# Gated linear attention layer: state products handed over two heads at a time, z units behind the last reads, weight parts in another order

## The reference, cut to what matters

```python
q, k, v, z, g_low = split(xn @ w_in)
log_a = log_sigmoid(g_low @ w_gate_up + b_gate) / 16
q_dec = q * dk ** -0.5 * exp(bcum); k_inv = k * exp(-bcum); k_dec = k * exp(b_last - bcum)
o_intra = tril(q_dec @ k_inv.T) @ v
def step(state, (qd, kd, vv, dec)):
    o = qd @ state
    state = state * dec[:, None] + kd.T @ vv
o = rms_norm(o_intra + o_inter, o_gain)
x = x + (o * silu(z)) @ w_out
```

## Time and profile before

| | us |
|---|---|
| median of 3 runs | 1286.72 |
| lowest, highest | 1285.8, 1289.21 |
| the profiled execution | 1288.8 |
| its span | 1287.1 |
| TensorE busy | 1108.6 (86%) |
| VectorE busy | 647.1 (50%) |
| ScalarE busy | 441.5 (34%) |
| granted clock of TensorE, mean | 0.961 |

### The profile page before, as it was taken

One profiled execution on the slowest core, in us unless ns is written; L12 is line 12 of the kernel. 1 busy time (PEld: TensorE's weight loads), 2 busy tenths in 40 slices (PEclk: granted clock), 3 DMA queues, 4 the chain that ended last, 5 costly groups with the idle time before them and its releaser, 6 DMA issues.

```text
span 1287.1 us, 19719 instructions
## 1 busy us (share of the span) xinstructions
PE 1108.6 (86%) x8083; PEld 817.1 (63%) x8083; DVE 647.1 (50%) x1279; ACT 441.5 (34%) x693; POOL 8.3 (1%) x36
## 2 busy tenths in 40 slices
PE   8999889897676758585858999999999989989998
PEld 8999767543131313130414789897779979868897
DVE  6886578420101111020203777767467966666685
ACT  5554334100000000000003556546356663255563
POOL 1000000000000000000000000000000000000000
PEclk9999999899898989898989999999999989899999
DMA  9576345999999999999998974354325530056600
GB/s 297 156 254 211 117 164 196 385 409 409 410 409 410 410 410 410 410 409 410 409 410 316 290 228 136 127 187 139 132 67 182 174 103 4 1 131 191 219 17 33
DMA packets 121045, 314.66 MB, mean 244 GB/s; under 512 B 17155, under 2 KB 19450, under 8 KB 120714
## 3 DMA queue, kind: packets, MB, share of 16 engines
q1 hardware_dynamic: 117904, 310.78, 65.9%
q0 software_dynamic: 352, 2.11, 0.4%
q10 hardware_dynamic: 2714, 0.71, 0.3%
HBM read 312.52 MB, written 1.06 MB: 244 GB/s over the span
## 4 chain that ended last, share of the span: by engine, by line
PE 59%; DMA 28%; DVE 7%; ACT 4%; issue 2%; SPq 1%; ACTq 0%; DVEq 0%
DMA ring<-in_w_up 18%; DMA ring<-in_w_down 10%; PE bank L2329 8%; PE bank L2322 7%; PE bank L2326 7%; PE bank L2308 6%; PE bank L2304 6%; PE bank L2311 6%; PE bank L2626 3%; PE bank L2649 2%; DVE w_l L1234 1%; PE bank L2237 1%; PE bank L2611 1%; PE bank L2732 1%; ACT w_h L694 1%
## 5 line engine op out<-in xcount | busy, mean ns | idle before, releaser
L1234 DVE TENSOR_TENSOR w_l<-ring,w_h 128x1024 fp32r<-128x1024 f32 x204 | 246.4, 1221 | 83.7 <-ACT w_h L694 82.3
L694 ACT ACTIVATE w_h<-ring 128x1024 fp32r<-128x1024 f32 x204 | 213.7, 1057 | 168.6 <-PE bank L2311 85.1
L2626 PE MATMUL bank<-ring,cm 128*32 128x512 f32 x880 | 135.4, 745 | 102.7 <-DMA ring<-in_w_gate 61.3
L2626 PEld LDWEIGHTS bank<-ring,cm 128*32 128x32 f32 x880 | 27.8, 120 | 208.6 <-DMA ring<-in_w_up 78.9
L2322 PE MATMUL bank<-w_h,hnT_h 128*128 128x512 f32 x480 | 135.1, 403 | 6.9 <-ACT hnT_h L789 2.7
L2329 PE MATMUL bank<-w_l,hnT_h 128*128 128x512 f32 x480 | 129.7, 392 | 5.7 <-DVE w_l L1234 5.7
L2326 PE MATMUL bank<-w_h,hnT_l 128*128 128x512 f32 x480 | 129.2, 391 | 0.0
L1717 DVE SCALAR_TENSOR_TENSOR cm<-cm,bank 128x512 f32<-128x512 f32 x8 | 5.5, 687 | 213.2 <-ACT cm L917 213.2
L2329 PEld LDWEIGHTS bank<-w_l,hnT_h 128*128 128x128 f32 x480 | 89.4, 188 | 27.7 <-DVE w_l L1234 8.8
L2322 PEld LDWEIGHTS bank<-w_h,hnT_h 128*128 128x128 f32 x480 | 86.5, 189 | 26.9 <-issue 4.2
L2326 PEld LDWEIGHTS bank<-w_h,hnT_l 128*128 128x128 f32 x480 | 90.3, 189 | 20.1 <-DVE hnT_l L1351 0.2
...
## 6 DMA issues: line engine op xcount, KB each, us to landing
...
```

What stands on the lines that cost most here:

```text
L694: af(part(w_h, u, width), w, ACT.Copy).then_inc(s["high_ready"], 1)
L1234: v.tensor_tensor(part(w_l, u, width), w, part(w_h, u, width).bitcast(F32), ALU.subtract).then_inc(s["low_ready"], 1)
L2626: x = mm(bank[a][CAP * e:CAP * (e + 1), :], m_xg[:, 2 * b + r, CAP * e:CAP * (e + 1)], expert_of(w, e)[:, r * FF:(r + 1) * FF], start=(b = ...
```

## The change

1. `turn_banks` of gla become 4, 6, 4, 6, the outputs' own banks; gdn keeps its own. 
2. `gla_st`, `gla_stc` and `gla_o` count two heads at a time; VectorE and ScalarE take each pair of heads when it is there.
3. `z_unit(1)` moves from behind `update(0)` to behind `update(1)`; `z_unit(2)` and `z_unit(3)` move behind the last state reads. Half of the first turned pair stands between them, half within `z_unit(3)` (`between`).
4. `out_gated` of the first tokens stands among the state updates; `token_tail` and `token_out` go, gla has its own lists and gdn keeps its order under the name `gdn_out`.
5. Parts of weights: VectorE's unit 14 stands ahead of the wait for the first exponential, unit 15 ahead of the third; ScalarE makes unit 15 before its exponentials. `high` and `low` of the last z and first output units move too.
6. In `add_projection`, for all layers that call it, the low parts stand ahead of L1386.

Left out below: the line numbers' shift, `turn_banks[name]` in two helpers, the removed `token_tail`, parameters handed through.

```diff
@@ -365,7 +365,7 @@
 xT = tiles(0, KD)
-turn_banks = (0, 1, 4, 5)
+turn_banks = {"gla": (4, 6, 4, 6), "gdn": (0, 1, 4, 5)}
 ROUTER_BANKS = (2, 3, 6, 7)
@@ -1026,6 +1026,7 @@
 if b == 1:
+    high(n + 4 * UNITS)
     act.wait_ge(s["gla_step"], 5)
@@ -1036,15 +1037,17 @@
 i.then_inc(s["gla_ktc"], 1)
-high(n + 5 * UNITS + PARTS + 2)
-out_squares(s["gla_o"], 0)
+high(n + 5 * UNITS + PARTS + 1)
+out_squares(s["gla_o"], 0, (0, 1), True)
+high(out + PARTS - 2)
+out_squares(s["gla_o"], 1, (0, 1), True)
 high(out + PARTS - 1)
-out_squares(s["gla_o"], 1)
+gains = [VCOL["gla_o_gain"], VCOL["gla_o_gain"] + 1]
+turned_high("gla", 0, gains)
 token_z("gla", 8, 1)
+turned_high("gla", 1, gains)
 high(out + PARTS)
-gains = [VCOL["gla_o_gain"], VCOL["gla_o_gain"] + 1]
-for p in range(3):
-    turned_high("gla", p, gains)
+turned_high("gla", 2, gains)
 high(out + PARTS + 1)
@@ -1380,11 +1365,11 @@
     x_lows(following, (0, 1))
+low(min(done + UNITS * (n + 1) + PARTS, done + 2 * UNITS + (2 if late else 0)))
 if k == 2 and following:
 ...
     link(v.tensor_scalar(ss[:, 10:12], ss[:, 8:10], 1.0 / D, EPS, ALU.mult, ALU.add))
-low(min(done + UNITS * (n + 1) + PARTS, done + 2 * UNITS + (2 if late else 0)))
 dve.wait_ge(s["unit_done"], done + UNITS * (n + 1))
@@ -1943,14 +1928,14 @@
 n = UNIT_BASE["gla"]
+low(n + 15)
 dve.wait_ge(s["gla_exp"], 1)
 ...
                        op0=ALU.mult, op1=ALU.mult)
-low(n + 14)
 dve.wait_ge(s["gla_exp"], 2)
 link(v.tensor_tensor(tf(28, 4), tf(4, 4), tf(28, 4), ALU.mult))
-low(n + 15)
+low(n + 16)
 dve.wait_ge(s["gla_exp"], 3)
@@ -1962,28 +1947,47 @@
+out, gains = UNIT_BASE["gla_out"], [VCOL["gla_o_gain"], VCOL["gla_o_gain"] + 1]
 for c in range(3):
     state, before = gla_states[c % 2], gla_states[(c + 1) % 2]
-    if c == 2:
+    for hf in (0, 1):
+        dve.wait_ge(s["gla_st"], 2 * c + hf + 1)
+        if c:
+            dve.wait_ge(s["gla_stc"], 2 * c)
+        for h in (2 * hf, 2 * hf + 1):
+            new = b2(2 + hf)[:, h % 2, :]
+            if c == 0:
+                x = v.tensor_copy(state[:, h, :], new)
+            else:
+                a = h * T + c * 64 + 63
+                x = v.scalar_tensor_tensor(out=state[:, h, :], in0=before[:, h, :], scalar=tf(20, 4)[:, a:a + 1],
+                                           in1=new, op0=ALU.mult, op1=ALU.add)
+        x.then_inc(s["gla_stc"], 1)
+    if c == 0:
+        low(n + 5 * UNITS + 4)
+    if c == 1:
         out_sums("gla", GLA_H, 0)
         out_roots(GLA_H, 0, 1.0 / GLA_DV)
-    dve.wait_ge(s["gla_st"], c + 1)
-    if c:
-        dve.wait_ge(s["gla_stc"], c)
-    for h in range(GLA_H):
-        new = b2(2 + h // 2)[:, h % 2, :]
-        if c == 0:
-            x = v.tensor_copy(state[:, h, :], new)
-        else:
-            a = h * T + c * 64 + 63
-            x = v.scalar_tensor_tensor(out=state[:, h, :], in0=before[:, h, :], scalar=tf(20, 4)[:, a:a + 1],
-                                       in1=new, op0=ALU.mult, op1=ALU.add)
-    x.then_inc(s["gla_stc"], 1)
-    if c < 2:
-        low(n + 5 * UNITS + 4 + c)
-low(n + 5 * UNITS + 6)
-dve.wait_ge(s["proj_copied"], PROJ_BASE["gla"] + 10)
-token_tail("gla", GLA_H, 8, [VCOL["gla_o_gain"], VCOL["gla_o_gain"] + 1])
+        dve.wait_ge(s["proj_copied"], PROJ_BASE["gla"] + 10)
+        out_gated(GLA_H, 8, 0, 0)
+    if c == 2:
+        out_gated(GLA_H, 8, 0, 1)
+out_sums("gla", GLA_H, 1)
+out_roots(GLA_H, 1, 1.0 / GLA_DV)
+for p in (0, 1):
+    out_gated(GLA_H, 8, 1, p)
+low(out + PARTS - 2)
+turned_low("gla", 0, gains)
+dve.wait_ge(s["proj_copied"], PROJ_BASE["gla"] + 12)
+for t in range(NT):
+    out_gated(GLA_H, 8, t, 2)
+turned_low("gla", 1, gains)
+low(out + PARTS - 1)
+for t in range(NT):
+    out_gated(GLA_H, 8, t, 3)
+turned_low("gla", 2, gains)
+low(out + PARTS + 1)
+turned_low("gla", 3, gains)
 add_projection(2)
@@ -2324,6 +2328,8 @@
     mm(dst, hnT_l[:, k, tt], wh[:, j, :], start=False, stop=False)
+if between is not None:
+    between()
 pe.wait_ge(s["low_ready"], u + 1)
@@ -2412,26 +2418,25 @@
         for j in (0, 1):
-            x = tr(b2(turn_banks[p])[:, j, t * P:(t + 1) * P], by_token(z0, t)[:, (2 * p + j) * P:(2 * p + j + 1) * P], ident[:])
+            x = tr(b2(turn_banks[name][p])[:, j, t * P:(t + 1) * P], by_token(z0, t)[:, (2 * p + j) * P:(2 * p + j + 1) * P], ident[:])
         if t == NT - 1:
 ...
-def token_out(name, z0):
-
-    pe.wait_ge(s["proj_copied"], PROJ_BASE[name] + 12)
+def gdn_out():
+
+    pe.wait_ge(s["proj_copied"], PROJ_BASE["gdn"] + 12)
     for t in range(NT):
         for p in (0, 1):
-            turned_pair(name, z0, p, (t,))
-            if name == "gdn" and (t, p) == (0, 1):
+            turned_pair("gdn", 16, p, (t,))
+            if (t, p) == (0, 1):
                 unread(16, 2)
-            if name == "gdn" and (t, p) == (1, 0):
+            if (t, p) == (1, 0):
                 unread(4, 2)
-    late = 1 if name == "gdn" else 0
-    out_projection(name, steps=range(1 + late))
-    turned_pair(name, z0, 2)
-    out_projection(name, steps=[1 + late])
-    turned_pair(name, z0, 3)
-    out_projection(name, steps=range(2 + late, 2 * UNITS))
+    out_projection("gdn", steps=range(2))
+    turned_pair("gdn", 16, 2)
+    out_projection("gdn", steps=[2])
+    turned_pair("gdn", 16, 3)
+    out_projection("gdn", steps=range(3, 2 * UNITS))
@@ -2814,7 +2820,8 @@
            vtm[lo:lo + 64, t, h * GLA_DV:(h + 1) * GLA_DV], start=True, stop=True)
-x.then_inc(s["gla_st"], 1)
+    if h % 2:
+        x.then_inc(s["gla_st"], 1)
@@ -2825,20 +2832,31 @@
 update(0)
-z_unit(1)
 for c in range(1, 4):
     t, lo = c // 2, 64 * (c % 2)
-    pe.wait_ge(s["gla_stc"], c)
     for h in range(GLA_H):
+        if h % 2 == 0:
+            pe.wait_ge(s["gla_stc"], 2 * c - 1 + h // 2)
         x = mm(b2(4 + 2 * t + h // 2)[lo:lo + 64, h % 2, :], cm[:, h, c * 64:(c + 1) * 64],
                gla_states[(c - 1) % 2][:, h, :], start=False, stop=(c % 2 == 1), skip_group_check=True)
-    if c % 2:
-        x.then_inc(s["gla_o"], 1)
+        if c % 2 and h % 2:
+            x.then_inc(s["gla_o"], 1)
     if c < 3:
         update(c)
-    if c % 2:
-        z_unit(2 + c // 2)
-token_out("gla", 8)
+    if c == 1:
+        z_unit(1)
+z_unit(2)
+pe.wait_ge(s["o_gated"], 2)
+turned_pair("gla", 8, 0, (0,))
+z_unit(3, lambda: turned_pair("gla", 8, 0, (1,)))
+pe.wait_ge(s["o_gated"], 4)
+turned_pair("gla", 8, 1)
+out_projection("gla", steps=[0])
+pe.wait_ge(s["proj_copied"], PROJ_BASE["gla"] + 12)
+turned_pair("gla", 8, 2)
+out_projection("gla", steps=[1])
+turned_pair("gla", 8, 3)
+out_projection("gla", steps=range(2, 2 * UNITS))
```

More of the change, by code:

```diff
@@ L2312, in channel_unit, with token_unit @@
                 x.then_inc(s["unit_done"], 1)
-            def token_unit(banks, u, m, first, last, pair=None, ends=(0, KD - 1)):
+            def token_unit(banks, u, m, first, last, pair=None, ends=(0, KD - 1), between=None):
                 wh, wl = part(w_h, u, BLK), part(w_l, u, BLK)
@@ L3038, in gdn @@
                     x.then_inc(s["gdn_o"], 1)
-                token_out("gdn", 16)
+                gdn_out()
             fox(0, 1, "fox0")
```

25 lines of the change are left out of this document (5 added, 20 removed).

## The result

The changed kernel takes **1275.07 us** (median of 4 runs, 1273.92 to 1275.55) against 1287.51 for the kernel before in the same session: ratio 0.9901, 95% interval 0.9888 to 0.9913. Faster, as forecast, but 2.4 us under the forecast and 0.4 under the range (1275.5 to 1281.8). The profiled execution took 1275.55 us, its span 1273.8, 13.3 less than the span of the kernel before.

The account below looks back on a forecast made before the run. TensorE, busy 86% of the span, was taken as the bound, its stops counting behind the mixture of experts. 2.4 + 4.4 + 2.4 = 9.2 us off the 1286.72 median gave 1277.5 us, range 1275.5 to 1281.8.

Parts of the forecast that it names:

- the view by stops: Behind the mixture of experts, TensorE's standing still counts: idle brackets of 2.18, 1.81, 1.35, 0.59 and 0.49 us, plus 0.3 start-up.
- Part A: gla's weight units 14 and 15: parts made sooner remove TensorE's stop at 891.13; 2.4 us, bounds 1.3 and 2.47.
- the thin place: Unit 15's low part in gla, ready 0.2 us before TensorE needs it; 0.1 us allowed for it.
- figure by the drain: gla's exponentials: with 2.66 us for table load plus drain, unit 15 comes 1.2 us late and about 1.2 is kept.
- Part B: gla's tail, first state product to fifth output unit: 37.36 us becomes 33.0; 4.4 us gained, bounds 2.2 and 4.7.
- rival 2: gla's tail waits for VectorE, five handoffs each slip 0.3 to 0.5 us, gain there 2.2: 1279.7 us; chance 0.16.
- Part C: Three passages between late layers: low parts ahead of L1386 save 0.8 us each, 2.4 in all; bounds 1.5 and 2.9.
- last sign of being wrong: If gdn or fox1 took another time than before by over 1 us, the cause would lie outside the sum.
- Rival 1: ScalarE's detour in gla costs more, exponentials over a microsecond later, unit 15's stop replaces unit 14's: 1278.6 us; chance 0.10.
- rival 3: No change that can be told, as two of three parts only move a wait: gain say 3 us, 1283.7; chance 0.08.
- Rival 4: Slower: a new TensorE wait in the changed part lets its clock fall to 1.2 GHz behind it; 1290.6 us; chance 0.03.
- Rival 5: The moved `low(n + 14)` did nothing before, unit 13 being already made among the scans; costs nothing, no chance given.

Follow-up runs that it names:

- four_heads: The changed kernel with states handed over between TensorE and VectorE only after all four heads, as before: 1279.63 us.
- old_banks: The changed kernel with gla's turned pairs in banks 0, 1, 4, 5 again, the first pair turned in one piece behind z unit 3: 1279.29 us.
- before_again: The kernel before, unchanged, run again for a second profile: 1290.31 us (one run).
- before_filled3: The kernel before with matmuls nobody reads in three of gla's TensorE stops, the 1.81 us stop left bare: 1287.17 us beside 1287.64.
- c_alone: The kernel before with only the low parts moved ahead of the small norm instruction in the passages: 1282.96 us.
- b_alone: The kernel before with only state products and updates by pairs, moved z units 2 and 3, and turned pairs in banks 4 and 6: 1280.53 us.
- without_a: The changed kernel with the order of weight units 14, 15 and 16 as before: 1279.49 us.
- a_alone: The kernel before with only unit 14's low part and unit 15's high part made sooner: 1286.19 us.

## Why the prediction was right and wrong

- **What bounds it, and the view by stops:** right. Every bracket named (2.18, 1.81, 1.35, 0.59, 0.49) is gone and none came in its place in gla or the passages.
- **Part A, 2.4 us:** 2.25 in the profile, with the thin place 0.15 late where 0.1 was allowed. The run of A alone could not resolve it. (The prediction's figure by the drain left out the 0.3 of start-up that its own lower bound has: A would have kept about 1, not 1.2.)
- **Part B, 4.4 us:** 4.39 in the profile, 32.96 us for 33.0; rival 2 (VectorE bounds the tail) did not come about though five handoffs had 0.3 us or less. four_heads and old_banks show that each half carries part of it.
- **Part C, 2.4 us: mis-sized.** It measured 3.5 (1.32, 1.31, 0.86), over its upper bound of 2.9 too. The step that failed is "That is 0.49 + 0.3 = 0.8 us" with "the row has its like at the two other passages": the price ends with TensorE's first late group. At gdn to fox1, where nothing near it waits, it was right (0.86). At the other two, the next layer's first group (0.2), the turning of x behind the late residual addition (0.2) and the turning's own length (0.1) came on top. The prediction had the residual addition only as a reason for its upper bound, with 0.5 us for all three passages.
- **gdn, taken as unchanged: the missing term, 2.8 us** in the profiled pair. Granted clocks of 0.50 to 0.79 from 1048 to 1102 us stood in the trace of the kernel before, of which the earlier trace rows shows only the first edge, and the sum treated the time behind the change as fixed. The prediction saw that "gdn's falls could shift either way" and gave it no price. Its last sign of being wrong, gdn off by over 1 us, is the one that came true. Against before_again's profile gdn gives 0.6 and gla's tail 2.9 more than geometry, 3.5 in all: the clock's share is there in each profile, its place is not fixed. The medians lie 12.4 us apart, 3.2 more than the sum of 9.2; the profiles, with 1.1 of part C and 2.8 of gdn less 0.15 of part A, explain 3.7.
- **Rival 1** out (1.30 us from load to use), **rival 3** out (12.4 us gained). **Rival 4** had the mechanism right and the kernel wrong: the falls sat behind the stops that the change takes away. **Rival 5:** nothing showed against it; not tried by itself.
- **The whole:** geometry 1.32 + 2.25 + 4.39 + 1.31 + 0.86 = 10.1 us, clock in gdn 2.8. By geometry alone the median would have been about 1286.7 - 10.1 = 1276.6, inside the range. The 0.4 us by which it fell out of the range are less than medians of this kernel differ by (1275.07, 1276.13, 1275.24), and so are no finding; the gain is one: 12.4, 11.9 and 12.4 us against the kernel before of each session, where 9.2 was forecast.

Open: which stop lets the clock fall in a given execution; why before_filled3 kept its 8.5 us of lost clock; gdn's low stretch at 1091 to 1101.5 us with the two stops filled; and why the medians of c_alone, b_alone and without_a moved 1.5 to 2 us more than geometry and a_alone's less.
